# RWKV scan: one of four PSUM copies per level of a triangular inverse given to VectorE instead of ScalarE

## The reference, cut to what matters

```python
def _wkv_scan(S0, decay, k, v, kk, a, r, reverse):
    ...
    def step(S, inp):
        w_t, k_t, v_t, kk_t, a_t = inp[:5]
        sa = jnp.einsum('bhvk,bhk->bhv', S, -kk_t)
        S = (S * w_t[:, :, None, :] + sa[..., None] * (kk_t * a_t)[:, :, None, :]
             + v_t[..., None] * k_t[:, :, None, :])
        y = jnp.einsum('bhvk,bhk->bhv', S, inp[5]) if len(inp) == 6 else None
        return S, y
```

## Time and profile before

| | us |
|---|---|
| median of 3 runs | 3779.27 (3776.16 to 3779.83) |
| the profiled execution: its own time | 3782.2 |
| its span in the trace | 3780.9 |
| TensorE busy over the span | 3527.5 (93%) |
| VectorE busy | 1656.9 (44%) |
| ScalarE busy | 1101.6 (29%) |
| GpSimd busy | 1389.0 (37%) |
| mean granted TensorE clock | 0.974 of 2.4 GHz |

### The profile page before, as it was taken

The page is one execution under the profiler, slowest core; times in us unless marked ns, Lnnn a source line. Parts: engine busy times, 40 slices in busy tenths (PEclk is TensorE's granted clock), DMA queues, the critical chain, the costliest instruction groups (busy, mean ns, idle before and its releaser), DMA issues.

```text
span 3780.9 us, 72300 instructions
## 1 busy us (share of the span) xinstructions
PE 3527.5 (93%) x31740; PEld 2276.1 (60%) x31740; DVE 1656.9 (44%) x2942; ACT 1101.6 (29%) x2087; POOL 1389.0 (37%) x1239
## 2 busy tenths in 40 slices
PE   7998899999999989898999998999889888889998
PEld 3755674344554555554555554456667677658887
DVE  1246561465531234444242426524566665333334
ACT  3153331322205633423000002114555455220002
POOL 1230640233312245665324333344344444144443
PEclk9999899999999999999999999999999999999999
DMA  5341005311112135311111111331000000122222
GB/s 191 131 141 34 2 14 190 128 48 48 45 56 73 34 125 178 122 34 45 56 56 62 61 50 50 106 113 51 16 17 17 17 17 4 61 67 88 90 90 67
DMA packets 196434, 263.77 MB, mean 70 GB/s; under 512 B 6135, under 2 KB 151671, under 8 KB 194072
## 3 DMA queue, kind: packets, MB, share of 16 engines
q1 hardware_dynamic: 188960, 241.74, 19.2%
q10 hardware_dynamic: 7160, 17.41, 1.2%
HBM read 246.55 MB, written 12.58 MB: 69 GB/s over the span
## 4 chain that ended last, share of the span: by engine, by line
PE 55%; ACT 6%; DVE 4%; issue 2%; POOL 1%; DMA 0%; ACTq 0%; DVEq 0%; POOLq 0%
PE ps L241 44%; PE ps L3274 2%; PE ps L794 2%; ACT mem L871 1%; PE ps L385 1%; PE ps L821 1%; PE ps L809 1%; PE ps L492 1%; DVE mem L852 1%; ACT mem L3209 1%; PE ps L3833 1%; PE ps L3816 1%; ACT mem L881 0%; PE ps L501 0%; PE ps L3824 0%
## 5 line engine op out<-in xcount | busy, mean ns | idle before, releaser
L241 PE MATMUL ps<-mem 64*64 64x64 f32 (+4 forms) x25120 | 2620.6, 296 | 101.0 <-ACT mem L3209 28.3
L241 PEld LDWEIGHTS ps<-mem 64*64 64x64 f32 (+1 forms) x25120 | 1704.1, 151 | 1024.6 <-issue 522.9
L3139 POOL TENSOR_TENSOR mem<-mem 128x256 f32<-128x256 f32 (+1 forms) x264 | 230.6, 887 | 323.0 <-ACT mem L3709 167.3
L889 POOL TENSOR_SCALAR mem<-mem 128x768 f32<-128x768 f32 (+2 forms) x128 | 219.0, 1724 | 199.8 <-DVE mem L855 199.7
L2384 POOL TENSOR_TENSOR mem<-mem 128x512 f32<-128x512 f32 (+1 forms) x80 | 100.7, 1259 | 443.2 <-PE ps L241 367.2
L2397 ACT ACTIVATE mem<-ps 128x384 f32<-128x384 f32 (+1 forms) x80 | 35.6, 446 | 777.9 <-PE ps L241 735.6
L599 POOL TENSOR_TENSOR mem<-mem 128x512 f32<-128x512 f32 (+1 forms) x72 | 75.2, 1060 | 419.5 <-ACT mem L594 416.4
L2408 DVE TENSOR_TENSOR mem<-mem,ps 128x384 f32<-128x384 f32 (+1 forms) x80 | 39.9, 499 | 414.5 <-PE ps L241 414.5
L3274 PE MATMUL ps<-mem 128*128 128x128 f32 x960 | 168.3, 292 | 14.7 <-DVE mem L3198 11.0
L3198 DVE TENSOR_TENSOR mem<-mem,ps 128x256 f32<-128x256 f32 (+1 forms) x220 | 110.4, 514 | 127.7 <-PE ps L241 126.9
L3207 ACT ACTIVATE mem<-ps 128x256 f32<-128x256 f32 (+1 forms) x220 | 101.3, 460 | 188.0 <-PE ps L3274 187.7
(11 more groups left out here) (322 smaller groups left out, 3976.8 us busy)
## 6 DMA issues: line engine op xcount, KB each, us to landing
mem<-i_mod_w SPq DMA_DIRECT2D x48, 1024.0 KB, 6.9
mem<-i_ffn_wg SPq DMA_DIRECT2D x22, 1024.0 KB, 5.3
mem<-i_ffn_wu SPq DMA_DIRECT2D x22, 1024.0 KB, 5.4
mem<-i_e_w_in SPq DMA_DIRECT2D x16, 1024.0 KB, 6.1
mem<-i_o_w_in SPq DMA_DIRECT2D x16, 1024.0 KB, 5.4
mem<-i_ffn_wd SPq DMA_DIRECT2D x16, 1024.0 KB, 5.0
mem<-i_e_mod_w SPq DMA_DIRECT2D x12, 1024.0 KB, 12.3
mem<-i_o_mod_w SPq DMA_DIRECT2D x12, 1024.0 KB, 7.2
```

The source lines that it names most:

```text
L241: ins = e.h.matmul(out, l, r, start=(i == 0), stop=(i == n - 1))
L889: K.pool.h.tensor_scalar(w, w, stat(i, o, 1), None, MUL).then_inc(*nm.up(tag, i, o))
L3139: K.pool.h.tensor_tensor(m3(self.slot(l)), self.lraw, bm(C(K, f"cm{self.d}", l, 64), 2 * self.np), MUL).then_inc(*self.mk.up(key, l))
```

## The change

Inverse64 gets a flag, split. With it, VectorE makes the T copy of each level (a tensor_copy of the turned matrix in bank b + 2), in stage A of its lane, and counts it on the lane's VectorE semaphore. ScalarE's T copy of the lane is left out, and its P copy stays. TensorE's u product waits for VectorE's T copy besides ScalarE's P copy, where it had only ScalarE's copies to wait for. The bank b + 2 counts as free when VectorE has copied it. Scan.inverse sets the flag for lane 1 alone. Lane 0, and both lanes of the delta net, stay as they are.

```diff
@@ levels (TensorE)
-            K.busy[tb] = [(self.cp, (key, "T", l))]
+            K.busy[tb] = [(self.u if self.split else self.cp, (key, "T", l))]
...
             claim(K, b, self.u, key, l)
+            if self.split:
+                K.pe.wait_ge(*self.u.at(key, "T", l))
             K.pe.wait_ge(*self.cp.at(key, "P", l))
@@ dve
         for l in range(1, 6):
+            if self.split:
+                K.dve.wait_ge(*self.pr.at(key, "v", l))
+                K.dve.h.tensor_copy(self.R["T"][:, 0:n * 128], K.ps[b + 2][:, 0:n * 128]).then_inc(*self.u.up(key, "T", l))
             yield
@@ act
         for l in range(1, 6):
-            K.act.wait_ge(*self.pr.at(key, "v", l))
-            K.act.h.activation(self.R["T"][:, 0:self.n], K.ps[turned][:, 0:self.n], ACT.Copy).then_inc(*self.cp.up(key, "T", l))
+            if not self.split:
+                K.act.wait_ge(*self.pr.at(key, "v", l))
+                K.act.h.activation(self.R["T"][:, 0:self.n], K.ps[turned][:, 0:self.n], ACT.Copy).then_inc(*self.cp.up(key, "T", l))
             K.act.wait_ge(*self.pr.at(key, "p", l))
@@ Scan.inverse
-        return Inverse64(K, key, before, L, d, d, m3(L["L"][:, 0:n * 128]), n, self.id64)
+        return Inverse64(K, key, before, L, d, d, m3(L["L"][:, 0:n * 128]), n, self.id64, split=d == 1)
```

More of the change, by code:

```diff
@@ L3115, with __init__ @@
 class Inverse64:
-    def __init__(self, K, key, before, R, lane, d, lraw, np_, id64, first=None, turned=None):
+    def __init__(self, K, key, before, R, lane, d, lraw, np_, id64, first=None, turned=None, split=False):
         self.K, self.key, self.before, self.R, self.lane, self.d = K, key, before, R, lane, d
+        self.split = split
         self.fb, self.tb = first, turned
```

## The result

The changed kernel takes 3792.72 us (median of 8 runs, 3788.53 to 3795.63) against 3779.28 us for the kernel before (8 runs, 3772.50 to 3782.21). The ratio is 1.0037, with a 95% interval from 1.0026 to 1.0048. That is 13.4 us slower by the medians, 9.8 to 18 us by the interval. The forecast was 3792.9 us.

A forecast was written before the change was run, and what follows sets the result against it. TensorE was taken as the bound, busy 625 of 707 us in the scan. Holds of 12.6 us plus 1 us of added wait took the profiled execution from 3782.2 to 3795.8 us, less 2.9 to the median: 3792.9 us, range 3777 to 3808.

The forecast's parts named there:

- No relief: Nearly all scan levels: P1 starts 0.07 us behind its product, so no gain; rival, relief everywhere, 3740 us, chance 0.06.
- Level 3: Level 3 of x = 1, where ScalarE is late: P1 starts 0.47 us earlier, the next turn gains 0.11 us.
- Level 2 and level 4: In x = 1: level 2's hold is hidden, 0.3 us to spare; level 4's copy holds L3586 and U0, 0.55 us.
- Level 5: Level 5 of x = 1: the copy holds the cumulative sum, U0 is 1.25 us late, 1.1 to 1.25 us lost.
- The holds together: Seven parts x = 1 with a front lose 1.8 us each: 12.6 us, between 7.7 and 15.4.
- TensorE's added wait: Second semaphore at lane 1's u products: 1 us taken, 0 to 5, at most 0.17 us at some 29 places.
- The sum: Whole kernel: 12.6 + 1 = 13.6 us, giving 3792.9 us, 0.36% slower; chance 0.58 of 3787 to 3796 us.
- The rival of the lower clock: In the scan, one more fall to 1.2 GHz per part adds 3.5 to 7 us: 3796 to 3800 us, chance 0.20.

The follow-up runs named there:

- not_45: The change without its copies in levels 4 and 5 of x = 1 (64 copies on VectorE), against the kernel before: 3786.19 us, ratio 1.0016.
- pe_wait: The kernel before, copies all on ScalarE, plus 80 already met TensorE waits ahead of lane 1's u products: 3784.42 us, ratio 1.0012.
- only_x0: The change kept in the parts x = 0 alone (40 copies of 256 columns), against the kernel before: 3785.33 us, ratio 1.0015.
- behind: The same 80 copies on VectorE, each placed behind the front's step of its round, against the kernel before: 3786.20 us, ratio 1.0018.
- pad_early: The kernel before plus 40 already met TensorE waits, all in the first two head pairs: 3787.74 us, ratio 1.0019.
- only_x1: The change kept in the parts x = 1 alone (40 copies of 512 columns), against the kernel before: 3790.79 us, ratio 1.0025.
- level3_three: The kernel before with lane 0's T and P and lane 1's T copies on VectorE, in level 3 of x = 1 only: 3765.08 us, ratio 0.9962.

## Why the prediction was right, and where not

**No relief.** Right. The distances of levels 1 to 4 of x = 0, outside the first pair, and of levels 1 and 2 of x = 1 stayed within 0.01 us with their copies off ScalarE. Nothing waited for those.

**Level 3.** Right: -0.10 us in the parts without a jump against -0.11 forecast, and in the kernel with T1 alone in this level the same.

**Level 2 and level 4.** Here the mechanism failed, though the number was met. I had level 2 as hidden and level 4 as L3586 (1.84 us) held by its copy, 0.55 us. The hold of level 2 is hidden from TensorE, but it sends GpSimd's L3612 off 0.81 us late, L3579 takes 2.43 us beside it in five of the seven parts, and U0 comes 0.8 to 0.9 us late with or without a copy in level 4 (not_45). L3586 took 1.24 us behind the copy in the part shown. The mean of +0.55 us equals the forecast by chance: the seven values run from -0.43 to +1.94 us.

**Level 5.** The mechanism was right: U0 late by 1.19 us against 1.25, and the solution products 1.17 us late in each of the seven parts. The distance to the next turn grew by less, 0.77 us in the part shown and 1.07 in the mean. In the part shown 0.27 us of the delay goes in the first gap behind it, 1.12 us long before and 0.83 after, and the rest where TensorE had waited for the handling of the solution products. I had written that I saw no wait behind level 5 that the delay could shrink, and these two are such. How much is caught up in the mean isn't shown, since pe_wait alone moves this distance by up to 1.8 us. In the sum it was 8.8 against 7.5 us.

**The holds together.** 12.6 us forecast, 3.8 + 7.5 - 1.1 = 10.2 us in the trace. By the runs, the change less pe_wait is 13.4 - 4.5 = 8.9 us, give or take 6 us by the two intervals.

**TensorE's added wait.** Undersized, 1 us against 4.5 (pe_wait, 1 to 8 by its interval) or 5.7 us (only_x0). And the mechanism was another. I had priced what one wait costs where it stands. In the levels it costs nothing (0.00 us in levels 1 to 4 of x = 0 behind the first pair). What the trace shows in its place is that TensorE's program is longer, so the places where it waits for its instructions fall elsewhere. My upper bound, 0.17 us for each of 29, gave 5 us for a wrong reason.

**The sum.** So the forecast of 3792.9 us met 3792.72 by luck, by two errors of opposite sign: the holds were 2.4 us too large and the waits some 3 to 5 us too small. And the holds hide the wrong reason for level 4. What these two leave over, 1 to 2 us, is far within the interval of the result, which is 8 us wide.

**The rival of the lower clock.** Over whole executions it isn't what made the change slower: the mean granted clock of its eight runs is 0.9728, against 0.9728 to 0.9734 in three sets of runs of the kernel before. Between runs of one kernel 0.001 goes with 2.2 us, so this is 0 to 1.5 us. Within the profiled scan it has a part. The time at 1.2 GHz between the first and the last turn was 20.5 us before and 34.1 after, in stretches of 3.4 us, and the one behind the new gap cost 1.7 us. In the experiments it was between 10 and 44 us, and least, 10 to 14 us, in the kernel behind and in the three that move lane 0's copies in level 3, which gained.

**What stays open.** The profiled gap of the sixth pair explains 1.6 to 3.6 us, and the runs with met waits alone give 4.5 and 7.2 us. I couldn't find all of the rest in single profiled executions: those of pe_wait and of pad_early are 3782.21 and 3778.83 us, 2 and 9 us under the medians of their own runs. A part of it goes with the clock: its mean over the runs of both is 0.9723 and 0.9724, and 0.9734 and 0.9733 in the kernel before beside them, some 2 to 2.6 us at 2.2 us for 0.001. That the waits lower the clock by more standing still is argued, not shown. Nor did I test other counts of added instructions, by which the same effect might be a gain, as it is in the second pair of only_x1 and pad_early. And no kernel has the copy in level 4 or in level 2 alone.

## What to carry to other kernels

Moving an operation to a less busy engine pays only where its old queue is the last thing that a consumer waits for. So first look whether the copy starts right behind its producer (0.07 us here), and if so leave it. On the new engine, what counts is not the operation's 0.69 us but its wait: an in-order engine that waits for a late producer holds back every step behind it, so put the moved step behind those that are ready. Follow such a hold on to the third engine: here one that TensorE never saw moved a step of GpSimd by 0.81 us, and through it VectorE and TensorE two levels later. Changes of 0.1 to 0.2% in a kernel bound by TensorE can come with instructions added anywhere ahead in its program (0.12% and 0.19% here). To know whether an edit earned them, run its waits alone as well.

## What the runs showed of the hardware that I had not expected

- TensorE stands still for 1 to 2 us at places where no semaphore is waited for, 18 times in the scan's 18,000 weight loads (21.0 us in 18 waits from 2660 to 3260 us in the kernel before, the longest 1.9). They come at one place in 256 of its instructions, and end 1.3 to 1.5 us behind the packet that loads the next ones. Adding 40 waits that were already met, in the first two of eight pairs, put one of them into dense work in the sixth pair, and the kernel took 0.19% [0.10, 0.28] longer.
- A step of VectorE on 128x756 elements took 0.94 us in one kernel (level3_three) and 2.43 us in another at the same place. With no two-input step of GpSimd beside it it took 0.93 or 0.94 us in every part; begun beside one, it ended 0.80 or 0.81 us behind that step's end in 109 of 112 cases over the fourteen kernels. This spread is larger than the copy whose cost was in question.
- VectorE's copy of 128x512 from PSUM took 0.69 us in the scan too, and that of 128x256 took 0.43 us at the shortest.
